# Layer 0's output products with three of eight chunks on split operands, x added in place by VectorE, and one buffer for the first attention's mixture

## The reference, cut to what matters

```
def diff_dsa_layer(x, norm_g, w_in, ..., w_o, rel_bias, layer, top_k):
    h = rms_norm(x, norm_g)
    qa, ka, va, qb, kb, vb, qi, ki, wi, gate = split_cols(h @ w_in, L0_SIZES)
    o_a = diff_attention(...)                      # 4 heads of 128, softmax minus lam * softmax
    o_a = rms_norm(o_a, subln_g) * (1.0 - lam_init)
    o_b = dsa_attention(...)                       # 8 heads of 64, on selected keys
    mix = jnp.concatenate([o_a, o_b], axis=-1)     # 1024 wide
    return x + (mix * jax.nn.silu(gate)) @ w_o
```

## Time and profile before

| | |
|---|---|
| time, median of 3 runs | 2450.6 us (2450.56 to 2453.54) |
| time of the profiled execution | 2449.3 us |
| its span | 2447.5 us |
| PE busy | 2318.4 us, 95% |
| DVE busy | 1706.0 us, 70% |
| ACT busy | 1347.6 us, 55% |
| POOL busy | 665.5 us, 27% |

### The profile page before, as it was taken

One profiled execution on the slowest core, in us unless ns is written; L12 is line 12 of the kernel. 1 busy time (PEld: TensorE's weight loads), 2 busy tenths in 40 slices (PEclk: granted clock), 3 DMA queues, 4 the chain that ended last, 5 costly groups with the idle time before them and its releaser, 6 DMA issues. The chain is left out here.

```text
span 2447.5 us, 36085 instructions
## 1 busy us (share of the span) xinstructions
PE 2318.4 (95%) x13451; PEld 1808.0 (74%) x13451; DVE 1706.0 (70%) x3281; ACT 1347.6 (55%) x2174; POOL 665.5 (27%) x582
## 2 busy tenths in 40 slices
PE   8999999999999999899998989999976999999998
PEld 7687887555557987677776878867755888888887
DVE  4899995678764216666766355257756898888887
ACT  5645222455555475556565342455553878777874
POOL 2545220011100002667777300012215122112211
PEclk9999999999999999999999989999987999999999
DMA  4122214011013232223333331211136999999996
GB/s 156 42 72 74 81 35 149 20 48 53 27 47 129 68 78 75 73 80 86 89 109 97 125 143 38 105 52 36 52 110 268 395 382 383 399 384 384 383 397 198
DMA packets 163511, 362.42 MB, mean 148 GB/s; under 512 B 34960, under 2 KB 82784, under 8 KB 163340
## 3 DMA queue, kind: packets, MB, share of 16 engines
q1 hardware_dynamic: 149964, 313.80, 35.3%
q0 software_dynamic: 13232, 46.25, 6.9%
q10 hardware_dynamic: 144, 0.07, 0.0%
HBM read 326.47 MB, written 38.86 MB: 149 GB/s over the span
## 5 line engine op out<-in xcount | busy, mean ns | idle before, releaser
L1176 ACT ACTIVATE a_pT<-ps 128x512 f32<-128x512 f32 (+3 forms) x176 | 79.5, 484 | 164.4 <-PE ps L1045 163.0
L4012 POOL DMA_INDIRECT out_dram<-m_q,e_token x15 | 35.8, 2384 | 443.6 <-DVE m_q L4215 443.6
L1188 ACT ACTIVATE a_p<-ps,a_stat 128x384 f32<-128x384 f32 (+7 forms) x192 | 129.1, 674 | 21.5 <-DVE a_stat L1272 15.3
L2977 ACT ACTIVATE l_lat<-ps,h_stat 128x384 f32<-128x384 f32 (+7 forms) x128 | 94.3, 741 | 76.3 <-DVE h_stat L3167 40.6
L1092 PE MATMUL ps<-l_wo,a_mixT 128*128 128x512 f32 x256 | 119.6, 593 | 0.0
L2557 POOL TENSOR_TENSOR ada_acc<-ada_acc,ada_w 128x384 f32<-128x384 f32 x112 | 116.6, 1041 | 8.8
L2987 ACT ACTIVATE h_pT<-ps 128x512 f32<-128x512 f32 (+2 forms) x192 | 83.5, 490 | 58.2 <-PE ps L2860 58.2
L3834 DVE TENSOR_TENSOR x_w2l<-x_raw,x_w2h 128x4096 fp32r<-128x4096 f32 x23 | 101.8, 4425 | 19.0 <-ACT x_w2h L3826 19.0
L3834 DVE TENSOR_TENSOR x_w1l<-x_raw,x_w1h 128x4096 fp32r<-128x4096 f32 x23 | 101.8, 4425 | 15.3 <-ACT x_w1h L3826 15.3
L3826 ACT ACTIVATE x_w2h<-x_raw 128x4096 fp32r<-128x4096 f32 x24 | 87.2, 3634 | 42.8 <-PE ps L4049 36.8
L3834 DVE TENSOR_TENSOR x_w0l<-x_raw,x_w0h 128x4096 fp32r<-128x4096 f32 x23 | 101.8, 4425 | 7.9 <-ACT x_w0h L3826 7.6
(11 more groups left out here) (745 smaller groups left out, 7192.3 us busy)
## 6 DMA issues: line engine op xcount, KB each, us to landing
x_raw<-in_w_gate SPq DMA_DIRECT2D x25, 2048.0 KB, 10.9
x_raw<-in_w_down SPq DMA_DIRECT2D x24, 2048.0 KB, 10.5
x_raw<-in_w_up SPq DMA_DIRECT2D x23, 2048.0 KB, 11.7
ada_w<-in_w_ada POOLq DMA_DIRECT2D x64, 384.0 KB, 3.8
m_ufT<-in_w_up SPq DMA_DIRECT2D x9, 2048.0 KB, 11.7
m_ufT<-in_w_down SPq DMA_DIRECT2D x8, 2048.0 KB, 13.0
l_raw<-in_e_w_in SPq DMA_DIRECT2D x28, 512.0 KB, 3.7
m_ufT<-in_w_gate SPq DMA_DIRECT2D x7, 2048.0 KB, 9.9
```

The source lines that it names most:

```text
L1188: nc.scalar.activation(self.p[2 * (u % 2) + side][:, 0:pair.width], self.S(u, side)[:, 0:pair.width], ACT.Exp, bias=self.stat[:, 1, s], sc ...
L2977: self.nc.scalar.activation(p[:, 0:w].rearrange("p (i n) -> p i n", i=2) if w > 512 else p[:, 0:w], self.S(u, side), ACT.Exp, bias=self.st ...
```

## The change

The first three of the eight chunks of the output product (`FrontSplit.N = 3`) use split operands: `l_wo_raw` (128 x 3 x 1024) is loaded ahead of the other five chunks, ScalarE makes its high part in the steps of pairs 1, 2 and 3, GpSimd the low part in place, before its first `norm_a`. In each block's last step ScalarE makes the high and VectorE the low part of the mixture's first 384 columns. TensorE does three products for each of these chunks (`FrontSplit.pe`). The first attention's mixture has one buffer (`a_front_mix`) in place of a part of both `mixT`. x is loaded into `a_y` itself, and VectorE adds the product to it (`dve_y`) where ScalarE copied and GpSimd added. Layer 1's first weights come into `kaT` for both halves, so their load waits for the last use of it.

```diff
     def act(self, e, at, m, i):
         y, col = at.y[m % 2][:], at.order[m]
         if self.gain is None:
-            e.wait_ge(at.y_done, m + 1)
+            e.wait_ge(at.y_half, 2 * m + 2)
             self.square(self.junk[0], y, 0, col).then_inc(self.squared, 1)
...
+        self.front, self.base = front, heads if front else 0
...
     def chunk_ready(self, e, n, c):
-        if c < self.heads:
+        if self.front and c < self.front.N:
+            e.wait_ge(self.front.mix_lows, n + 1)
+        elif c < self.heads:
             e.wait_ge(self.moved["dve"], self.turns[self.per * n + self.heads + 2, "mix"].moved)
         else:
             e.wait_ge(self.mixed, self.per * n + max(0, c - (KD - self.per)) + 1)
@@ -1088,11 +1091,15 @@
                 self.chunk_ready(e, n, c)
             if self.split:
                 last = self.split.pe(e, n, h, c)
+            elif self.front and c < self.front.N:
+                self.front.pe(e, n, h, c)
             else:
-                last = nc.tensor.matmul(t.ps[:, 7, :], self.lhs_out(n, self.order[n], c), self.w_out[:, c, h * 512:(h + 1) * 512],
+                last = nc.tensor.matmul(t.ps[:, 7, :], self.lhs_out(n, self.order[n], c), self.w_out[c][:, h * 512:(h + 1) * 512],
                                         start=c == 0, stop=c == KD - 1)
             if c == KD - 1:
                 last.then_inc(self.made, 1)
+            elif self.front and h == 1 and c == self.heads - 1:
+                last.then_inc(self.front.used, 1)
...
         e.wait_ge(self.turned, x.n + 1)
+        if n:
+            e.wait_ge(self.front.used, n)
         flat = lambda ap: ap[:, 0:self.heads, :].rearrange("p c n -> p (c n)")
-        self.k.nc.vector.scalar_tensor_tensor(flat(self.mixT[n % 2]), self.t.ps[:, x.bank, 0:self.heads * P], self.gain[:],
+        self.k.nc.vector.scalar_tensor_tensor(flat(self.front.mix), self.t.ps[:, x.bank, 0:self.heads * P], self.gain[:],
...
+    def dve_y(self, e, pieces):
+        for n, h, c in pieces:
+            if c < KD - 1:
+                continue
+            y = self.y[n % 2][:, h * 512:(h + 1) * 512]
+            e.wait_ge(self.made, 2 * n + h + 1)
+            if h == 0:
+                self.add_end(e, n)
+            self.k.nc.vector.tensor_tensor(y, y, self.t.ps[:, 7, :], ALU.add).then_inc(self.y_half, 1)
...
     def act(self, e):
         self.k.nc.scalar.activation(self.warm[:], self.t.ident[:, 0:1], ACT.Exp)
         for _, nxt, cur in self.steps():
             if nxt is not None:
                 self.act_exp(e, nxt, 0)
-            if cur:
+            if cur and not self.front:
                 self.act_y(e, self.pieces(cur - 1))
             if cur is not None:
                 for g in range(len(self.pairs[cur].groups)):
@@ -1213,12 +1232,15 @@
                     self.rows.act(e, self, cur)
                 if self.split:
                     self.split.act(e, self, cur)
+                if self.front:
+                    self.front.act(e, self, cur)
...
         for far, nxt, cur in self.steps():
+            if cur and self.front:
+                self.dve_y(e, self.pieces(cur - 1))
...
+                if self.front:
+                    self.front.dve(e, self, cur)
                 self.dve_move_mix(e, cur)
                 self.dve_out(e, cur)
...
+        if self.front:
+            self.dve_y(e, self.pieces(len(self.pairs) - 1))
...
+class FrontSplit:
+
+    N = 3
+
+    def __init__(self, k, mix):
+        self.nc, self.mix = k.nc, mix
+        self.raw_in, self.highs, self.lows = k.sem("l0_front_in"), k.sem("l0_front_highs"), k.sem("l0_front_lows")
+        self.mix_highs, self.mix_lows, self.used = k.sem("l0_front_mix_highs"), k.sem("l0_front_mix_lows"), k.sem("l0_front_used")
+
+    def lay(self, k, t):
+        self.t, scope = t, k.scope
+        self.high = k.sb("l0_woh", [P, self.N, D], F32R)
+        with ExitStack() as under:
+            k.scope = under
+            self.raw = k.sb("l0_wo_raw", [P, self.N, D])
+        k.scope = scope
+        self.low = k.sb("l0_wol", [P, self.N, D], F32R)
+        self.mix_h, self.mix_l = (k.sb(f"l0_front_mix{part}", [P, self.N, P], F32R) for part in "hl")
+
+    def load(self, e, w):
+        e.dma_start(self.raw[:], rows(w)[:, 0:self.N, :]).then_inc(self.raw_in, 16)
+
+    def pe(self, e, n, h, c):
+        if n == h == 0:
+            e.wait_ge(self.lows, c + 1)
+        cols = slice(h * 512, (h + 1) * 512)
+        for part, (x, w) in enumerate(((self.mix_h, self.high), (self.mix_h, self.low), (self.mix_l, self.high))):
+            self.nc.tensor.matmul(self.t.ps[:, 7, :], x[:, c, :], w[:, c, cols], start=c == part == 0, stop=False)
+
+    def act(self, e, at, u):
+        if 0 < u <= self.N:
+            e.wait_ge(self.raw_in, 16)
+            self.nc.scalar.activation(self.high[:, u - 1, :], self.raw[:, u - 1, :], ACT.Copy).then_inc(self.highs, 1)
+        n, i = divmod(u, at.per)
+        if i == at.per - 1:
+            e.wait_ge(at.moved["dve"], at.turns[at.per * n + at.heads + 2, "mix"].moved)
+            if n:
+                e.wait_ge(self.used, n)
+            self.nc.scalar.activation(self.mix_h[:], self.mix[:, 0:self.N, :], ACT.Copy).then_inc(self.mix_highs, 1)
+
+    def dve(self, e, at, u):
+        n, i = divmod(u, at.per)
+        if i == at.per - 1:
+            e.wait_ge(self.mix_highs, n + 1)
+            self.nc.vector.tensor_tensor(self.mix_l[:], self.mix[:, 0:self.N, :], self.mix_h[:].bitcast(F32), ALU.subtract).then_inc(self.mix_lows, 1)
+
+    def pool(self, e):
+        for c in range(self.N):
+            e.wait_ge(self.highs, c + 1)
+            self.nc.gpsimd.tensor_tensor(self.low[:, c, :], self.raw[:, c, :], self.high[:, c, :].bitcast(F32), ALU.subtract).then_inc(self.lows, 1)
...
-        def add_end(e, n, y):
+        def add_end(e, n):
             e.wait_ge(x_in[n % 2], 16 * (n // 2 + 1))
-            return nc.gpsimd.tensor_tensor(y[:], y[:], xb[n % 2][:], ALU.add)
-
-        at = PairAttention(k, "a0", t, pairs, A_DIM ** -0.5, True, lambda n, b, c: at.mixT[n % 2][:, c, :], None,
+
+        at = PairAttention(k, "a0", t, pairs, A_DIM ** -0.5, True,
+                           lambda n, b, c: front.mix[:, c, :] if c < A_HEADS else at.mixT[n % 2][:, c - A_HEADS, :], None,
                            (w_in, 16), g_in, add_end, gate=gT, heads=A_HEADS, gain=subln, gained=gained,
-                           tiles={"p": p, "mixT": mixT, "y": y}, sums=RowSums(k, "l0", t, junk), busy=2, ahead=start)
+                           tiles={"p": p, "mixT": mixT, "y": y}, sums=RowSums(k, "l0", t, junk), busy=2, ahead=start, front=front)
...
+        mixT.append(k.sb("a0_mixT1", [P, KD - A_HEADS, P]))
+        wo = k.sb("l0_wo", [P, KD - FrontSplit.N, D])
+        at.w_out = [None] * FrontSplit.N + [wo[:, c, :] for c in range(KD - FrontSplit.N)]
+        front.lay(k, t)
...
-        first_rooms = [x[:, 0:KD // 2 * n].rearrange("p (k n) -> p k n", n=n)
-                       for x in (k.sb("l0_room", [P, EARLY0])[:], kaT[:].rearrange("p h n -> p (h n)"))]
+        first_rooms = [kaT[:].rearrange("p h n -> p (h n)")[:, i * KD // 2 * n:(i + 1) * KD // 2 * n].rearrange("p (k n) -> p k n", n=n)
+                       for i in range(2)]
...
-            e.dma_start(wo[:], rows(a["e_w_o"][0])).then_inc(w_in, 16)
+            front.load(e, a["e_w_o"][0])
+            e.dma_start(wo[:], rows(a["e_w_o"][0])[:, FrontSplit.N:, :]).then_inc(w_in, 16)
             for n, b in enumerate(order):
                 if n >= 2:
-                    e.wait_ge(at.y_done, n - 1)
-                e.dma_start(xb[n % 2][:], a["x"][0][b * P:(b + 1) * P, :]).then_inc(x_in[n % 2], 16)
+                    e.wait_ge(at.y_stored[n % 2], 16 * (n // 2))
+                    e.wait_ge(at.sums.squared, n - 1)
+                e.dma_start(y[n % 2][:], a["x"][0][b * P:(b + 1) * P, :]).then_inc(x_in[n % 2], 16)
                 if n + 1 < NB:
                     for half in range(2):
                         at.load_gate(e, n + 1, half, t.gateT_d)
                 if n == NB - 1:
                     first.load_gain(e, a["o_norm_col"])
+                    e.wait_ge(at.exped, 2 * (n * at.per + A_HEADS))
                     first.load(e, 0)
...
             nc.gpsimd.tensor_scalar(subln[:], subln[:], 1.0 - LAM_INIT, None, ALU.mult).then_inc(gained, 1)
+            front.pool(e)
             for n in range(NB):
                 norm_a(e, n)
-                if n:
-                    at.pool(e, n - 1)
         return at
...
```

More of the change, by code:

```diff
@@ L929, in __init__ @@
     def __init__(self, k, tag, t, pairs, scale, tiled, lhs_out, w_out, w_in, gate_in, add_end, q_ready=None, mover=None,
-                 gate=None, aside=None, heads=0, gain=None, gained=None, tiles={}, sums=None, rows=None, split=None, busy=0, ahead=None):
+                 gate=None, aside=None, heads=0, gain=None, gained=None, tiles={}, sums=None, rows=None, split=None, busy=0, ahead=None, front=None):
```

(24 more changed lines are left out.)

9 lines of the change are left out of this document (2 added, 7 removed).

## The result

The changed kernel takes 2463.9 us (median of 5 runs, 2460.6 to 2464.8); the kernel before took 2450.6. The ratio is 1.0054, 95% interval 1.0041 to 1.0067: slower by about 13 us, where 8 were forecast. The profiled execution took 2460.6 us with a span of 2458.8, 11.3 more than that of before.

A forecast was written before the change was run, and what follows sets the result against it. TensorE, busy almost throughout, was taken as the bound. Products -3.0, wait and conversions +5.4, VectorE held +4.5, clock +0.5 and tail +0.6 gave +8.0 us: profiled 2457.3, median placed at 2458, range 2451 to 2464.

The forecast's parts named there:

- The start: First block: ScalarE's wait for the raw load and VectorE held by GpSimd together cost about 10 us.
- The exp: First block: ScalarE's exp starts 4.75 us late behind load and conversion; two more conversions add 0.34 each, sum 5.4.
- The held instructions: First block: GpSimd's three subtractions hold VectorE's instructions until they end, 4.5 us, bounds 0 and 7.05.
- The products: Output products in the pairs: split operands save 0.30 us per half, 4.2 over 14 halves, 3.0 kept.
- The adds: Steps inside the pairs: VectorE's 14 adds of 0.69 us are hidden in its wait for scores; far bound 9.7.
- the steady part: Pairs behind the start: the split products' saving shows there, -3.0 us.
- My sign of being wrong: Wide blocks: the prediction is wrong if VectorE's adds make TensorE wait there; no size given.
- The tail: Last output products: TensorE waits 1.4 us for VectorE's add, split products save 0.39 per half; net +0.6 us.
- The clock: First block: a pause of 5 us may lower TensorE's granted clock for longer, 0.5 us, bounds 0 and 2.
- (b): First block: only the wait costs, GpSimd's subtractions miss VectorE's two-input instructions; +3.5 us, 2454; chance 0.24.
- (d): Output products: every split chunk costs 0.65 us, saving 10 us, all realised; -6.4 us, 2444; chance 0.06.
- (c): First block: later load or TensorE staying at 1.2 GHz adds 3.4 or 1.5 us, up to 2463; chance 0.12.

The follow-up runs named there:

- e1: Changed kernel with GpSimd's three subtractions of the weights' low parts replaced by fills with zero; 2460.6 us.
- e5: Changed kernel with VectorE's 14 adds inside the pairs replaced by ScalarE's copies of before, x's addition left out; 2457.2 us, ratio 1.0020 to the kernel before.
- e11: Changed kernel plus filler products on TensorE: 30 and 2 ahead of the turns of pairs 2 and 3, 2, 4 and 12 behind pairs 5 to 7; start +9.46 us.
- e2: Changed kernel with the raw weight load issued ahead of SP's wait for the stored gates and the two gate loads; 2459.5 us.
- e6: Changed kernel without the split (N = 0, no raw load, conversions or low parts), VectorE's adds kept; 2454.7 us, ratio 1.0013 to the kernel before.
- e7: Changed kernel, conversions moved to pairs 5 to 7, subtractions behind the first normalisation, VectorE's adds in the step that ends a half; 2450.1 us, ratio 0.9989.
- e8: e7 plus 4, 6 and 16 filler products on TensorE behind the sums of the first block's pairs 5 to 7; 2447.5 us, ratio 0.9978.
- e10: e7 plus 2, 4 and 12 filler products on TensorE behind the sums of the first block's pairs 5 to 7; ratio 0.9994.
- e9: Changed kernel plus fillers: 48 and 4 ahead of the turns of pairs 2 and 3, 4, 6 and 16 behind pairs 5 to 7; start +12.59 us.

## Why the prediction was right and wrong

**The start: right in sum and in both mechanisms, 10.2 us against 10.4 forecast.** The exp was 6.08 late, not 4.75: the load landed at 415.9, not at 414.5, inside the bounds. The two further conversions added 0.26 each, not 0.34. The held instructions lost 4.35 by their durations (3.7 shown by e1), against 4.5. That makes 6.08 + 0.52 + 4.35 = 10.95 at 429.87, where the exp of 418.92 stands. 0.7 is given back by the end of the second block's first eight scores: these took 1.99 us, before's 2.32, and another 0.34 lies in the transposes, fillers and sum just ahead of them, where before's clock was down (0.79 from 421 to 427 us).

The Trainium skill's "SBUF — State Buffer", section "Who interferes with whom", says that two SBUF inputs on VectorE and a read by GpSimd lock each other out. The trace agrees: L1307 took 1.68 us beside each of the two subtractions it met. The section also says that a GpSimd instruction that only writes SBUF does not do this to a two-input one; no run here shows that, as e1's fills overlap L1307 by only 0.13 us.

**The products: right.** 1.50 us for two chunks, 2.18 for three. By the Trainium skill's "TensorE: Matmul & The Clock Gate", section "Back-to-back issue gap", a chunk would take 0.65, an estimate of three times its 216 ns; the trace has 0.70 for a further one and doesn't agree. The section calls this formula one for an isolated product that over-counts in a stream at 512 columns; here the stream is slower than it, not faster. In the pairs they gain 3.9 us (e5), against 4.2 worked out before I took 1.2 off.

**The adds: this step failed.** "The adds stand at a step's start, where VectorE waits for scores, so they are hidden." The forecast for the steady part was -3.0; it was +1.20, 4.2 us off, which is more than the stage's whole error (11.8 against 8.0). For the narrow blocks I had taken off 1.2 us, without working it out; it measured 5.1. I had asked whether VectorE has time for an add, and found its wait of 1.00 us in a wide block. I hadn't asked when TensorE needs the bank back. In narrow blocks VectorE reaches the add so late that TensorE could have begun the next half up to 0.8 us before, and waits. Before, ScalarE had done this early. The adds cost 1.20 + 3.93 = 5.1 us inside the pairs beside the split and 2.8 without it; TensorE's visible waits for them, 3.4 us, all lie in blocks of 640 keys or fewer. My own text named this wait for the tail and charged 1.4 (1.31 measured), but for none of the other halves. My sign of being wrong, adds that make TensorE wait in the wide blocks, named the wrong blocks; the sign for the steady part, 2 to 4 us less than before, failed.

**The tail: right.** +0.40 against +0.6.

**The clock.** Forecast 0.5 for a pause of 5 us. It was 0.50 from 415 to 428 us in the first block, where it cost next to nothing as far as e11 shows, and 0.86 from 440 to 452, where it cost about 1.3 (e2). Before had falls of its own (e6 without one was 2.15 us shorter), so the difference between the two is small, and no step failed here. Each kernel was profiled once; whether a kernel's falls repeat from execution to execution isn't shown.

**The rivals.** (b) and (d) are out: VectorE was held all three times, and a chunk costs 0.70 to 0.79. The median lies just past (c)'s "up to 2463", but not for its reasons: the load landed inside its bounds, and the low clock of the first block cost next to nothing. The profiled executions differ by 11.3 us, and the stage's 11.8 covers that; the medians differ by 13.3, and for the rest, which is within what whole times scatter, I have no place. That the range, up to 2464, still holds 2463.9 is luck: the term for the steady part had the wrong sign, and the range was not drawn for that.

**What remains of the change.** With conversions late and adds early the stage is 3.7 to 5.0 us shorter than before (the last figure with fillers), and the whole kernel 0.1 to 0.2% faster (e7 0.9989, e8 0.9978), with one of three not told from no change (e10 0.9994). Their order by whole time is not that by the stage, and stays unexplained.

## What to carry to other kernels

When work moves to another engine, ask not only whether that engine has time, but who waits for the result and how long after its input is ready it will be reached there; repeat it for every step shape, the narrow ones first. Conversions of constants belong where the chain has cover, and a shared resource is dear on the chain: three holds, 4.35 us long, cost 3.7 us in the first four pairs, and one of 1.70 us a few pairs later cost at most 0.3. Read a small change from marks inside the trace, where 0.25 us could be told here outside the stretches in which the clock falls, and leave the whole time to say whether it matters.

## What was not expected of the hardware

The granted clock of this stretch differs between kernels in which TensorE does nearly the same work: 1.00 without a fall (e6), 0.79 from 421 to 427 and 0.72 from 434 to 440 (before), 0.50 from 415 to 428 around the end of an idle time of 7.89 us (changed kernel). Behind one and the same wait of 3.2 us the eight scores took 1.99 us in four kernels and 2.79 to 3.79 in five. In e11 TensorE had 64 filler records in the long wait and 1.66 us idle, and the clock fell to 0.50 all the same, from 424 to 428; in e9, with 100 records and no idle time before the turn, it stayed at 1.00. What decides it the runs don't show.

A fill by GpSimd, which reads nothing, held VectorE's COPY of one SBUF tensor (0.50 us instead of 0.23, from 424.69 to 425.19, the fill ending at 425.11). The Trainium skill's "SBUF — State Buffer", section "Who interferes with whom", lists the copy among the instructions that can take the shared ports, which agrees.
